# A decoder step on one Trainium2 core: where the rows of the first norm's values start, and how many columns the mixing strips take

## The reference

```
h = rmsnorm(x, norm1_g);  z = h @ w_in                 # D_MODEL 2048
u, cg, bg, q, k, v, o, gates, g_a, g_b = split(z)
a_out = bg * shortconv(cg * u)                          # causal, width 3
b_out = sigmoid(o) * mlstm(q, k, v, gates)              # 8 heads
x = x + (sigmoid(g_a) * a_out + sigmoid(g_b) * b_out) @ w_out
h2 = rmsnorm(x, norm2_g)
up = shortconv(h2 @ w_up)                               # 2 * 5632 columns
x = x + (silu(up[D_FF:]) * up[:D_FF]) @ w_down
y = rmsnorm(x, norm_f_g)
```

## Time and profile before

| | us |
|---|---|
| median of 3 runs | 1697.74 (1697.56 to 1698.33) |
| the profiled execution | 1698.14 |
| its span, first to last instruction | 1696.4 |
| TensorE busy | 1684.1 (99%) |
| VectorE busy | 1194.5 (70%) |
| ScalarE busy | 767.4 (45%) |
| GpSimd busy | 477.6 (28%) |

### The profile page before, as it was taken

The page is one execution under the profiler, slowest core; times in us unless marked ns, Lnnn a source line. Parts: engine busy times, 40 slices in busy tenths (PEclk is TensorE's granted clock), DMA queues, the critical chain, the costliest instruction groups (busy, mean ns, idle before and its releaser), DMA issues.

```text
span 1696.4 us, 37171 instructions
## 1 busy us (share of the span) xinstructions
PE 1684.1 (99%) x13712; PEld 1677.6 (99%) x13712; DVE 1194.5 (70%) x1901; ACT 767.4 (45%) x916; POOL 477.6 (28%) x501
## 2 busy tenths in 40 slices
PE   9999999999999999999999999999999999999997
PEld 8999999999999999999999999999999999999997
DVE  5875857677585766758688877777555777777554
ACT  6545435353443535344445554544333334334443
POOL 4422415242241524224333222222000222222220
PEclk9999999999999999999999999999999999999999
DMA  8788786868878687877766666666666666566663
GB/s 208 189 223 199 199 212 172 212 176 219 192 190 217 166 216 180 212 192 193 195 180 181 190 178 183 180 180 174 183 183 181 180 179 183 174 184 175 186 178 121
DMA packets 591309, 318.80 MB, mean 188 GB/s; under 512 B 17756, under 2 KB 586060, under 8 KB 589156
## 3 DMA queue, kind: packets, MB, share of 16 engines
q1 hardware_dynamic: 578564, 292.99, 64.0%
q10 hardware_dynamic: 10592, 21.57, 5.1%
q0 software_dynamic: 2064, 2.92, 0.8%
HBM read 305.09 MB, written 12.78 MB: 187 GB/s over the span
## 4 chain that ended last, share of the span: by engine, by line
PE 99%; DMA 0%; ACT 0%; DVE 0%; SPq 0%; issue 0%; ACTq 0%; DVEq 0%
PE strip L1526 32%; PE strip L1530 32%; PE strip L1534 32%; PE aux L1408 1%; PE strip L1457 0%; DMA w_raw<-in_w_in 0%; PE aux L1587 0%; PE aux L1477 0%; PE strip L1470 0%; PE aux L1617 0%; PE aux L1616 0%; PE aux L1630 0%; PE aux L1621 0%; PE aux L1614 0%; PE aux L1622 0%; PE aux L1613 0%
## 5 line engine op out<-in xcount | busy, mean ns | idle before, releaser
L714 ACT ACTIVATE w_hi<-w_raw 128x1024 fp32r<-128x1024 f32 x557 | 588.7, 1060 | 786.1 <-PE strip L1534 753.1
L987 DVE TENSOR_TENSOR w_lo<-w_raw,w_hi 128x1024 fp32r<-128x1024 f32 x556 | 710.3, 1282 | 295.0 <-ACT w_hi L714 292.6
L1526 PE MATMUL strip<-xh,w_hi 128*128 128x268 f32 (+1 forms) x2016 | 291.0, 286 | 0.0
L1530 PE MATMUL strip<-xl,w_hi 128*128 128x268 f32 (+1 forms) x2016 | 290.0, 286 | 0.0
L1534 PE MATMUL strip<-xh,w_lo 128*128 128x268 f32 (+1 forms) x2016 | 290.0, 286 | 0.0
L1526 PEld LDWEIGHTS strip<-xh,w_hi 128*128 128x128 f32 x2016 | 265.1, 188 | 0.2
L1530 PEld LDWEIGHTS strip<-xl,w_hi 128*128 128x128 f32 x2016 | 265.2, 188 | 0.0
L1534 PEld LDWEIGHTS strip<-xh,w_lo 128*128 128x128 f32 x2016 | 265.2, 188 | 0.0
L1526 PE MATMUL strip<-x2h,w_hi 128*128 128x266 f32 x1408 | 200.2, 284 | 0.0
L1530 PE MATMUL strip<-x2l,w_hi 128*128 128x266 f32 x1408 | 199.9, 284 | 0.0
L1534 PE MATMUL strip<-x2h,w_lo 128*128 128x266 f32 x1408 | 199.9, 284 | 0.0
(11 more groups left out here) (330 smaller groups left out, 1525.5 us busy)
## 6 DMA issues: line engine op xcount, KB each, us to landing
w_raw<-in_w_in SPq DMA_DIRECT2D x256, 512.0 KB, 4.5
w_raw<-in_w_up SPq DMA_DIRECT2D x176, 512.0 KB, 4.1
w_raw<-in_w_down SPq DMA_DIRECT2D x64, 512.0 KB, 4.1
w_raw<-in_w_out SPq DMA_DIRECT2D x32, 512.0 KB, 4.7
w_raw<-in_w_down SPq DMA_DIRECT2D x32, 384.0 KB, 3.4
out<-c_st ACTq DMA_DIRECT2D x8, 1024.0 KB, 7.1
c_st<-in_state_mlstm_C ACTq DMA_DIRECT2D x7, 1024.0 KB, 10.8
rb<-scratch_rows ACTq DMA_DIRECT2D x8, 270.0 KB, 5.1
```

The source lines that it names most:

```text
L714: act.activation(w_hi[:, slot, :], w_raw[:, slot, :], ACT.Copy).then_inc(hi_done, 1)
L987: v.tensor_tensor(w_lo[:, slot, :], w_raw[:, slot, :], w_hi[:, slot, :].bitcast(f32), ALU.subtract).then_inc(lo_done, 1)
L1526: pe.matmul(bank[b][:, 0:c1 - c0], w_hi[:, slot, w], rh[:, k0 + k, c0:c1], start=(first and k == 0), stop=False)
L1530: pe.matmul(bank[b][:, 0:c1 - c0], w_hi[:, slot, w], rl[:, k0 + k, c0:c1], start=False, stop=False)
```

## The change

The rows of `xh` and `xl` become 288 columns (XW), 1152 bytes, with the 280 values from column 6 (XO) of the row on, and the tiles begin 32 bytes into their block, so that the first value lies at 56 modulo 64. Every reader and writer adds XO. The block grows by 1536 bytes a partition, and `pre_f` leaves its own place and lies over tiles that are dead by then. Strip 0 and the strips of `back` other than 4, 5, 10 and 11 take 266 columns from M0 on (at 48 modulo 64); `take` gets the strip's first column.

```diff
+    XO = 6
+    XW = 288
...
-        sb("x_parts", [P, 2 * KT * NT])
-        xh = nc.alloc_sbuf_tensor_at("xh", [P, KT, NT], f32r, offset=x_parts)
-        xl = nc.alloc_sbuf_tensor_at("xl", [P, KT, NT], f32r, offset=x_parts + KT * NT * 4)
+        sb("x_parts", [P, 2 * KT * XW + P])
+        xh = nc.alloc_sbuf_tensor_at("xh", [P, KT, XW], f32r, offset=x_parts + 32)
+        xl = nc.alloc_sbuf_tensor_at("xl", [P, KT, XW], f32r, offset=x_parts + 32 + KT * XW * 4)
         x2h = nc.alloc_sbuf_tensor_at("x2h", [P, KT, MW], f32r, offset=x_parts + 32)
-        x2l = nc.alloc_sbuf_tensor_at("x2l", [P, KT, MW], f32r, offset=x_parts + 32 + KT * NT * 4)
+        x2l = nc.alloc_sbuf_tensor_at("x2l", [P, KT, MW], f32r, offset=x_parts + 32 + KT * XW * 4)
...
-        pre_f = sb("pre_f", [P, 2 * FT, NS])
...
+        cursor[0] = v_1_0
+        pre_f = at("pre_f", [P, 2 * FT, NS])
...
-                act.activation(xh[:, k, :], x_bank[k % 6][:, 0:NT], ACT.Copy, scale=vecs[:, k:k + 1])\
+                act.activation(xh[:, k, XO:XO + NT], x_bank[k % 6][:, 0:NT], ACT.Copy, scale=vecs[:, k:k + 1])\
...
-            def take(u, b, out, c0, width, from_c=C0):
+            def take(u, b, out, c0, width, from_c=M0):
...
-                        take(u0 + i, i // 2 % RING, out[:, :], c0, width)
+                        take(u0 + i, i // 2 % RING, out[:, :], c0, width, c0)
...
-                c0 = C0 if s == 0 else 0
+                c0 = M0 if s == 0 else 0
...
-                        mm = pe.matmul(bank[s][:, 0:NT - c0], w_hi[:, 2 * s + k // KU, w], xt[:, k, c0:NT],
+                        mm = pe.matmul(bank[s][:, 0:NT - c0], w_hi[:, 2 * s + k // KU, w], xt[:, k, XO + c0:XO + NT],
...
             def mix_strip(n, s, c0, c1, between=None):
-                strip(n * 16 + s, n * HEAD_U + 2 * s, 2 * s, s % RING, xh, xl, c0, c1, (), between)
+                strip(n * 16 + s, n * HEAD_U + 2 * s, 2 * s, s % RING, xh, xl, XO + c0, XO + c1, (), between)
...
-                    mix_strip(n, s, C0 if s == 0 else 0, NT, spread_r if first and s == 2 else None)
+                    mix_strip(n, s, M0 if s == 0 else 0, NT, spread_r if first and s == 2 else None)
...
-                    mix_strip(n, s, C0, NT)
+                    mix_strip(n, s, C0 if s in (4, 5, 10, 11) else M0, NT)
```

More of the change, by code:

```diff
@@ L217, in hybrid_decoder_step @@
         k_lo = at("k_lo", [P, 2, DK], f32r)
+        v_1_0 = cursor[0]
         v_1 = at("v_1", [P, DV])
@@ L1028, in _ @@
                 v.wait_ge(xh_done, k + 1)
-                v.scalar_tensor_tensor(out=xl[:, k, :], in0=x_bank[k % 6][:, 0:NT], scalar=vecs[:, k:k + 1],
-                                       in1=xh[:, k, :].bitcast(f32), op0=ALU.mult, op1=ALU.subtract)\
+                v.scalar_tensor_tensor(out=xl[:, k, XO:XO + NT], in0=x_bank[k % 6][:, 0:NT], scalar=vecs[:, k:k + 1],
+                                       in1=xh[:, k, XO:XO + NT].bitcast(f32), op0=ALU.mult, op1=ALU.subtract)\
                                         .then_inc(xl_done, 1)
@@ L1470, in first_lo_part @@
                     mm = pe.matmul(bank[s][:, 0:NT - c0], w_lo[:, 2 * s + h, (k - h * KU) * P:(k - h * KU + 1) * P],
-                                   xh[:, k, c0:NT], start=False, stop=(last and k == KT - 1))
+                                   xh[:, k, XO + c0:XO + NT], start=False, stop=(last and k == KT - 1))
                 return mm
@@ L1476, in gates @@
                     for t, xt in enumerate((xh, xl)):
-                        mm = pe.matmul(aux[1][0:GM, 0:NT], gws[:, k, :], xt[:, k, :], start=(k == 0 and t == 0),
+                        mm = pe.matmul(aux[1][0:GM, 0:NT], gws[:, k, :], xt[:, k, XO:XO + NT], start=(k == 0 and t == 0),
                                        stop=(k == KT - 1 and t == 1))
```

## The result

The changed kernel takes 1706.13 us (median of 6 runs, 1705.66 to 1706.56) against 1698.03: a ratio of 1.0046, interval 1.0036 to 1.0057. It is slower by 8 us, where 0.6 less was forecast. The time lies beyond the range (1702.5).

What follows compares the result with a forecast made beforehand. TensorE was taken to bound the kernel, through its matmuls' start-to-start distance. Terms -1.3 (the 71), +0.7 (the 32), 0 (the 23) and 0 (first stage) summed to -0.6 us: median 1697.1, range for 8 in 10 1691.5 to 1702.5.

Steps and rivals of the forecast that it cites:

- rival 3: Mixing strips: the place within 128 bytes counts and 112 is the dear half; +6.2 us, 1703.3; chance 0.07.
- the 32: Mixing strips 4, 5, 10, 11 of 8 heads, staying at 268 columns, now from 40: +0.022 each, +0.7 us.
- Rival 1: The 32 and the 23: starts 8 bytes off 16 cost one piece more, 1.8 ns; +3.6 us (1701.3), far end 1706; chance 0.22.
- the 71: Mixing strips going from 268 to 266 columns from 48: 0.018 us less each, -1.3 us, bounds 6.8 each way.
- The 23: Mixing strips that stay at 280 columns and now start at 56: taken as 0, from 1.4 us less to +4.0.
- rivals 2: Mixing strips: the place within 128 bytes counts and 112 is the cheap half; -7.4 us, 1689.7; chance 0.13.

Runs made afterwards that it cites:

- The first table: Kernel before, with 96 TensorE matmuls per layout (266, 268, 280 columns; several strides, starts) behind its end; 266 in rows of 1088 from 48 took 5.84 us per 48.
- the second table: Kernel before, with matmuls of 264 to 282 columns at 16 places, rows 1152 bytes apart, behind its end; 264-column means 5.804 and 5.914 us per 48.
- e1_columns: Kernel before with only the columns changed: 71 strips take 266 columns from column 14 in the old 1120-byte rows; 1701.30 us, ratio 1.0023.
- c1_xo4: Changed kernel with the values from column 4 of the row and not 6; 1694.67 us, ratio 0.9978 against the kernel before.
- c2_down: c1_xo4 with the down strips' input hh, hl in rows of 1152 bytes, first used column at 64 modulo 128; 1693.88 us, ratio 0.9969.

## Why the prediction was wrong

**Right:** what bounds the kernel. TensorE's start-to-start distance was the whole of it, no engine came onto the path, the weight rings' move by 1536 bytes and `pre_f`'s cost nothing behind the mixing strips (93.47 us for the output strips, 127.36 for the first 16 down strips), and distances, not mean durations, gave the prices. Also that how a start counts could not be read from four layouts.

**The step that failed first:** "The nearest row is the 266 columns of `mh`, same width, same start modulo 64: 5.858 - 5.840 = 0.018 us each". `mh`'s rows lie at two places modulo 128 in turn, the new ones at one, and seen from the weights this one is dear: 5.922. The text named this difference and allowed 2 ns per matmul for it; it was 1.7 above `mh`. But it then took the middle as likeliest, and gave the dear half (rival 3) a chance of 0.07. This term was +3.9 and not -1.3 us. The first table holds 40 layouts of 266 columns: 17 of them take 5.92, and `mh`'s 5.84 is their lowest price. It is the good case, not a neutral one.

**The second:** for the 32, "5.840 plus two columns = 5.880, because the uniform 48 is the nearest start". The table's price for that place is 6.00, and 6.00 to 6.09 was measured: +4.3 us in all (forecast +0.7). The price before was mis-read as well. The cut of the earlier trace rows starts at a strip 11 and holds no strip 4, 5 or 10, so its 5.858 was never the price of half of the 32. Strips 4, 5, 10 and 11 of head 1, before and then after:

```profile
147.09:153.04 5.95, 5.95 (x50) 1.00 0.99 262
154.70:160.64 5.94, 5.94 (x51) 1.00 0.64 162
184.08:189.94 5.86, 5.86 (x50) 1.00 0.63 161
192.94:198.79 5.85, 5.85 (x50) 1.00 0.82 228
...
147.04:153.04 6.00, 6.00 (x50) 1.00 0.84 228
154.70:160.78 6.08, 6.08 (x51) 1.00 0.61 155
184.47:190.47 6.00, 6.00 (x51) 1.00 0.64 169
193.46:199.53 6.07, 6.07 (x50) 1.00 0.72 199
```

Strip 4 rose by 0.05, 5 and 10 by 0.14, 11 by 0.22. How much of it is a piece of 16 bytes more is not shown: the second table's mean gap for 268 columns is 0.9 ns per matmul, 0.044 us per strip, against the 1.8 ns priced.

**Rival 1** doesn't carry the result. Its far end, 1706, is the measured time by chance: it left the 71 at -1.3. The 23 that it made dearer by at least 0.09 us each rose by 0.02. Together the 32 and the 23 rose by 4.8 us, which is rival 1's nearer price, but nearly all of it lies in the 32. Rival 3's direction is what the 71 did: +3.9 us, where it has +5.5. The two were taken as alternatives, though nothing shut either out where the other held. That is why the range ended too soon. The times given for rivals 2 and 3 also take the forecast's 0.6 us off twice: -7.4 and +6.2 from 1697.7 are 1690.3 and 1703.9.

A slip without weight: TensorE's wait of 2.1 us is not at the tail. It ends 2.1 us after the span's start, before the first matmul.

**What the columns would do:** by two columns alone a strip would fall by 0.04 us (2 x 0.417 x 48 ns). e1_columns has this edit with the old rows kept, and it rose by 0.06. There the start moved too, by 8 bytes, so the columns' own share can't be seen under the place's.

## What to carry to other kernels

A matmul's price in this 32-bit form is its columns plus 16 to 38 cycles (264 columns from 144, 266 in rows of 1216 from 32), and the second part depends on where input rows and weights lie towards each other and, in some layouts, on what ran before. Don't infer a layout's price from one that shares its start modulo 64: put a table of strips behind the kernel's end, with its own strides and places, read the start distances, and choose by them. Then look whether the kernel repeats the price: c1_xo4 did to 0.01 us in the strips cut, c2_down gained 2.4 us of 8.3. If two unknown costs can both be there at once, add them for the range.

## What was not expected of the hardware

- 264 columns cost 5.601 us per 48 from 144 and from 192 (116.7 ns, 280 cycles), 5.92 eight bytes on from 144.
- One layout held two prices, 5.86 and 5.96, for whole strips on end. Which one differed with the single matmul before it (64 to 78 columns), in one execution.
- Behind a short matmul the first start distance was 195 to 213 ns, some 0.08 us more than the next ones.
- Most prices lie on steps of 0.04 us per 48 matmuls, two cycles of 2.4 GHz each (5.84, 5.88, 5.92, 6.00, 6.08): 157 of the 215 prices of the two tables, within 0.002 us, 58 of them at 5.92. Others, as 5.86, 5.95 and 5.97, don't.
